# Layer 1's key gather ahead of its first weights; layer 0's parameters and states on ScalarE's queue

## What is computed

```python
for l in range(2):                      # layers
    h = rms_norm(x, norm_g[l])
    a_val, a_glu, a_gate, b_val, b_gate, q, k, v, c_gate = split(h @ w_in[l])   # 384,384,384,256,256,384,384,384,384
    u  = a_val * sigmoid(a_glu)         # conv over 31 positions; the samples use state_conv[l]
    ya = silu(layer_norm(dwconv(concat(conv_buf, u)))) * silu(a_gate)
    yb = pool_linear(trailing_means(concat(pool_buf, b_val)) - b_val) * silu(b_gate)   # samples: state_pool[l]
    q, k = rope(rms_norm(q)), rope(rms_norm(k))
    o  = dilated_attention(q, concat(cache_k, k), concat(cache_v, v))  # distances 0..128, 4*(0..128), 16*(0..128)
    x  = x + concat(ya, yb, o * silu(c_gate)) @ w_out[l]
    # outputs also: conv and pool tails, and both caches of every sample moved on by one position
```

## Time and profile before

| | us |
|---|---|
| median of 3 runs | 431.8 (431.1 to 432.26) |
| the profiled execution | 428.37 |
| its span | 426.5 |
| TensorE busy | 353.0 (83%) |
| VectorE busy | 231.9 (54%) |
| ScalarE busy | 103.4 (24%) |
| mean granted clock of TensorE | 0.943 of 2.4 GHz |
| moved by DMA | 158.06 MB, mean 371 GB/s |

### The profile page before, as it was taken

How to read it: one execution, slowest core, us unless ns; L and a number is a source line. 1 busy time by engine, 2 the same in 40 slices (tenths; PEclk the granted TensorE clock), 3 DMA queues, 4 the chain that set the end, 5 groups by cost and what they waited for, 6 DMA issues and landing times.

```text
span 426.5 us, 4489 instructions
## 1 busy us (share of the span) xinstructions
PE 353.0 (83%) x1552; PEld 273.1 (64%) x1552; DVE 231.9 (54%) x522; ACT 103.4 (24%) x243; POOL 38.1 (9%) x70
## 2 busy tenths in 40 slices
PE   1480099999859896999997999999658988999993
PEld 1360088888647675556886888888446754558872
DVE  1232008997997677542104259989987686341110
ACT  4200010153314342141102101443124332320113
POOL 0698000000000000000000000000009000000000
PEclk9997589999986999999998999999969998999998
DMA  8999999999999999999999999999989999999995
GB/s 295 399 420 418 358 406 343 372 392 415 353 378 416 418 413 373 345 337 362 423 412 379 416 411 412 365 415 382 314 306 380 390 377 339 336 329 325 329 335 231
DMA packets 47301, 158.06 MB, mean 371 GB/s; under 512 B 3861, under 2 KB 16351, under 8 KB 46703
## 3 DMA queue, kind: packets, MB, share of 16 engines
q0 software_dynamic: 22592, 100.62, 63.8%
q1 hardware_dynamic: 16040, 34.40, 22.2%
q10 hardware_dynamic: 8646, 22.76, 13.9%
HBM read 154.90 MB, written 104.42 MB: 608 GB/s over the span
## 4 chain that ended last, share of the span: by engine, by line
PE 57%; DVE 16%; DMA 14%; SPq 6%; ACT 2%; issue 2%; ACTq 0%; DVEq 0%
PE pj L544 28%; PE pj L683 13%; DMA st_pool<-in_state_pool 7%; DMA kv<-in_cache_v_win 7%; PE psc L615 7%; DVE kv L1046 4%; DVE ssc L1049 4%; DVE yc L1106 3%; SPq L394 3%; PE ptr L470 2%; PE ps L492 2%; SPq L371 1%; SPq L386 1%; DVE qk L983 1%; PE ps L666 1%
## 5 line engine op out<-in xcount | busy, mean ns | idle before, releaser
L544 PE MATMUL pj<-hT,w 128*128 128x264 f32 x800 | 195.3, 403 | 2.8 <-DVE hT L968 2.8
L544 PEld LDWEIGHTS pj<-hT,w 128*128 128x128 f32 x800 | 157.5, 200 | 34.5 <-issue 7.0
L1106 DVE SCALAR_TENSOR_TENSOR yc<-u_ext,par,yc 128x256 f32<-128x256 f32 x180 | 76.2, 481 | 2.8 <-DVE u_smp L996 0.6
L683 PE MATMUL pj<-mix,w 128*128 128x264 f32 x256 | 59.2, 386 | 0.0
L683 PEld LDWEIGHTS pj<-mix,w 128*128 128x128 f32 x256 | 48.5, 190 | 8.2
L462 POOL DMA_DIRECT2D out<-in_cache_k_win x32 | 18.5, 586 | 292.1 <-issue 277.7
L1176 DVE TENSOR_TENSOR xT<-xT,pj 128x264 f32<-128x264 f32 x16 | 6.9, 430 | 53.6 <-PE pj L683 53.6
L994 DVE SCALAR_TENSOR_TENSOR u_ext<-ex,pj 128x256 f32<-128x256 f32 x6 | 2.5, 422 | 48.6 <-ACT ex L791 48.6
L615 PE MATMUL psc<-kv,spm 128*48 128x384 f32 x80 | 27.3, 492 | 0.4 <-DMA kv<-in_cache_v_win 0.4
L791 ACT ACTIVATE ex<-pj 128x264 f32<-128x264 f32 x22 | 8.6, 391 | 76.2 <-PE pj L544 68.0
L897 ACT ACTIVATE hT<-xT 128x264 f32<-128x264 f32 x16 | 6.8, 423 | 66.1 <-DVE xT L1176 66.1
(11 more groups left out here) (169 smaller groups left out, 333.9 us busy)
## 6 DMA issues: line engine op xcount, KB each, us to landing
out<-in_cache_k_win POOLq DMA_DIRECT2D x32, 1512.0 KB, 90.5
out<-in_cache_v_win POOLq DMA_DIRECT2D x32, 1512.0 KB, 95.8
w<-in_w_out ACTq DMA_DIRECT2D x2, 4096.0 KB, 27.1
w<-in_w_in ACTq DMA_DIRECT2D x1, 4608.0 KB, 29.8
kv<-in_cache_k_win SPq DMA_DIRECT2D x32, 144.0 KB, 24.6
w<-in_w_in ACTq DMA_DIRECT2D x3, 1536.0 KB, 27.8
kv<-in_cache_v_win SPq DMA_DIRECT2D x32, 144.0 KB, 18.1
w<-in_w_in SPq DMA_DIRECT2D x1, 4608.0 KB, 29.9
```

What stands on the lines that cost most here:

```text
L544: last = nc.tensor.matmul(pj[n % RING][:, 0:T], wbuf[buf][:, k, col:col + P], hT[:, k, :], start=(k == 0), stop=(k == KD - 1))
L683: last = nc.tensor.matmul(pj[n % RING][:, 0:T], w1[:, k, m * P:(m + 1) * P], mix[:, k, :], start=(k == 0), stop=(k == KD - 1))
L1106: last = V.scalar_tensor_tensor(out=yc[:, t, 0:SEQ], in0=x_w, scalar=par[:, ROW_CW + w * CT + t:ROW_CW + w * CT + t + 1], in1=yc[:, t, 0:S ...
```

## The change

- The parameters of layer 0 are issued from ScalarE's queue, ahead of its first computation; its states from the same queue behind the three squares, then the q weights, which now wait for `a_val_in`.
- `st0` and `st1` move from behind projections 1 and 2 to behind 5 and 6, in both layers.
- POOL's bulk copies wait for `a_gate_in` in place of `a_val_in`.
- In layer 1, SP issues the key gather ahead of the `a_` weights; it waits only for the seventh `sc_full` of layer 0. In layer 0 it stays behind the pool weights.

```diff
 _behind = {
-    1: ["st0"], 2: ["st1"], 8: ["sconv"],
+    5: ["st0"], 6: ["st1"], 8: ["sconv"],
...
             weights(0, w0, 0, "w_in", COL["a_val"], 2 * C_CONV, "a_val_in")
-            params(0)
             sp.dma_start(cst[:, early:], const[:, early:]).then_inc(const_in, 16)
 
             for l in range(DEPTH):
                 if l > 0:
+                    sp.wait_ge(S["sc_full"], nth(l - 1, "sc_full", NH + 1))
+                    gather("k", l, "k_in")
                     sp.wait_ge(S["pj_full"], nth(l - 1, "pj_full", NPROJ))
                     weights(l, w0, 0, "w_in", COL["a_val"], 3 * C_CONV, "a_in")
                 else:
                     weights(l, w0, 2 * C_CONV, "w_in", COL["a_gate"], C_CONV, "a_gate_in")
-                if l == 0:
-                    states(l)
...
-                sp.wait_ge(x_copied, XROUNDS)
-                if l > 0:
-                    sp.wait_ge(S["sc_full"], nth(l - 1, "sc_full", NH + 1))
-                gather("k", l, "k_in")
+                if l == 0:
+                    sp.wait_ge(x_copied, XROUNDS)
+                    gather("k", l, "k_in")
...
-            pool.wait_ge(S["a_val_in"], 16)
+            pool.wait_ge(S["a_gate_in"], 16)
...
             nc.scalar.preload_act_table_set(LOG_SET)
 
+            for r0, name, pat in ((ROW_CW, "conv_w", "o w (t c) -> (o w t) c"), (ROW_CB, "conv_b", "o (t c) -> (o t) c"),
+                                  (ROW_LG, "ln_g", "o (t c) -> (o t) c"), (ROW_LB, "ln_b", "o (t c) -> (o t) c"),
+                                  (ROW_PS, "pool_scale", "o (t c) -> (o t) c"), (ROW_NG, "norm_g", "o (t c) -> (o t) c")):
+                src = ins[name][bass.ds(0, 1)].rearrange(pat, c=P)
+                act.dma_start(prow[r0:r0 + src.shape[0], :], src).then_inc(S["par_in"], 16)
+            for r0, name in ((ROW_QN, "q_norm_g"), (ROW_KN, "k_norm_g")):
+                for h in range(2):
+                    act.dma_start(prow[r0:r0 + 1, h * HD:(h + 1) * HD], ins[name][bass.ds(0, 1)]).then_inc(S["par_in"], 16)
+
             act.wait_ge(x_in, 32)
             act.wait_ge(early_in, 16)
...
+            act.dma_start(st_conv[:, :, :], ins["state_conv"][bass.ds(0, 1)].rearrange("o (r s) w c -> (o s w) r c", r=2)
+                          ).then_inc(S["st_in"], 16)
+            act.dma_start(st_pool[:, :], ins["state_pool"][bass.ds(0, 1)].rearrange("o s w c -> (o s w) c")).then_inc(S["st_in"], 16)
+            act.wait_ge(S["a_val_in"], 16)
             weights(0, w1, 0, "w_in", COL["q"], 3 * C_ATT, "q_in")
```

More of the change, by code:

```diff
@@ L379, in params @@
             def params(l):
-                if l > 0:
-                    sp.wait_ge(S["tr_full"], nth(l - 1, "tr_full", TR["par"] + 1))
+                sp.wait_ge(S["tr_full"], nth(l - 1, "tr_full", TR["par"] + 1))
                 for r0, name, pat in ((ROW_CW, "conv_w", "o w (t c) -> (o w t) c"), (ROW_CB, "conv_b", "o (t c) -> (o t) c"),
@@ L391, in states @@
             def states(l):
-                if l > 0:
-                    sp.wait_ge(S["tr_full"], nth(l - 1, "tr_full", TR["st1"] + 1))
+                sp.wait_ge(S["tr_full"], nth(l - 1, "tr_full", TR["st1"] + 1))
                 sp.dma_start(st_conv[:, :, :], one("state_conv", l).rearrange("o (r s) w c -> (o s w) r c", r=2)
```

## The result

The changed kernel takes 447.9 us in the median (444.29 to 455.79, 4 runs) against 431.45 of the kernel before beside it: a ratio of 1.0385, interval 1.0329 to 1.0442. That is slower, as forecast, but by 16.5 us where 7.3 was the sum, and outside the range (431 to 444.5). The profiled execution took 447.06, its span 445.3; from profile to profile that is 18.7 us more than before, where the medians lie 16.5 apart. Every ratio here is worked out from fast runs alone (that of 455.79 us is not among them), and beside the first four experiments only two of seven runs of the kernel before were fast.

What follows compares the result with a forecast made beforehand. TensorE's projections bound the kernel nearly everywhere, with full DMA queues deciding its waits. Layer 0 -27.5, hole ahead of layer 1 +34.6 and clock +0.2 sum to +7.3 us on 431.8: 439 us, range 431 to 444.5.

Steps and rivals of the forecast that it cites:

- its wait moves as it is: Value gather of layer 0: TensorE's wait shifts unchanged with the earlier layer 0, sample values done at 166.7, before 194.2.
- just hidden: Bulk copies start at about 29, end 5.3 us later at about 425, before the last rows of y at 428.
- I take 0.5 off it: Start of layer 0: 0.5 us off the 4.9 us gain, for small packets sharing engines; first projection at about 18.1.
- 4.4 us booked for the parameters' move: Start of layer 0: parameters on ScalarE's queue bring the first projection earlier, gain 4.9 us less 0.5.
- The states: Layer 0: states land within a few us, no hole before projection 2; projection 8 ends at 53.1, 27.5 us earlier.
- the second rival: Layer 0: states land late as before, at 52, costing 10.7 us of the gain; 450 us, chance 0.04.
- I book nothing: Layer 0's key gather lands by 71, VectorE asks at 77.5; six us of cover, so no cost.
- Gather and weights, 72.0 us: Ahead of layer 1: gather issued at 166.7, weights behind it landed at 238.7; TensorE stands 34.6 us.
- 189.2 + 0.2: Layer 1: 189.2 us from its start to the last issue, as before, plus 0.2 us for the clock behind the hole.
- the third rival: End of kernel: bulk copies end last because their start moves by 14.2 us; 441 us, chance 0.09.
- The first rival: Layer 1: weights land in time, layer 0's gain stays; 428 to 430 us, chance 0.11; no change, another 0.11.

Runs made afterwards that it cites:

- the first four experiments: Changed kernel with weights first in layer 1 (1.0201); kernel before with keys first (1.0802); changed kernel with copies early (1.0315); changed kernel with weights first, copies early (1.0141).

## Why the prediction was wrong

The sign and the place were right: the gather ahead of the weights makes a hole ahead of layer 1, ended by `w<-in_w_in`, larger than what layer 0 gains. The order alone, added to the kernel before, costs 8%; taken from the changed kernel, it moves the end of compute by 43.7 us. Without copies it costs nothing, as even turns between small rows and the copies' large ones are what makes the gather slow. The size was wrong in three terms of compute and in the term of the copies. Two steps failed: for the time, "its wait moves as it is", the largest of the three; as reasoning, the copies that stay "just hidden".

- *First projection, "I take 0.5 off it"*: 19.39, not 18.1. The small DMAs took 1.6 us from the prompt and the identity matrix, shown by putting them back. **1.3 us.** Of the 4.4 us booked for the parameters' move, 0.5 were its own.
- *The states*: right, and the second rival falls. They landed within 8.3 us, and projection 8 ended at 54.7. Layer 0 was 26.0 us ahead there, against 27.5.
- *Layer 0's keys, "I book nothing"*: right in effect, with little room. The last piece landed at 48.4 + 28.8 = 77.2, where 71 was forecast, and VectorE asked at 79.0: 1.8 us of cover, not six. With the copies early this cover was gone, and VectorE waited.
- *The value gather, "its wait moves as it is"*: **the largest of the terms, 6.6 us.** It landed 33.6 us behind its last issue, against 29.4, and TensorE's 16 matmuls behind it took 7.47 us at a mean granted clock of 0.71, against 5.33 us at 1.00 before. L614 is at 174.7, not at 166.7. How far this is the change's is open: in four other kernels with the late start of the copies (weights first with one semaphore and with 11, the parameters on SP, the changed kernel with 11) that landing took 31.1 to 31.4 us, and the output projection started at 172.2 to 173.8, against 177.4 here. Some 2 us of the landing are common to them; the rest was seen in this execution only.
- *Gather and weights, 72.0 us*: 75.2 here, 73.2 and 74.6 with the parameters on SP and with 11 semaphores. **3.2 us.** The share was right (39 packets per us beside v's weights, where 39.7 was forecast); q1 moved 2008 packets in 179 to 217, about the gather's 2048, and at 39 per us the weights' 1040 were out by about 244, but they landed at 249.9, where 2 us were booked. The last rows straggled: q1 still moved 0.15, 0.09 and 0.03 MB in 244 to 246, 246 to 248 and 248 to 250.
- 1.3 + 6.6 + 3.2 = 11.1 of the 11.3 us by which layer 1 started later than 238.7. From its start on, 189.6 us to the last issue, against 189.2 + 0.2. So 7.3 + 11.3 + 0.2 = 18.8 us, the difference of the spans; that the medians differ by 2.3 less is because the median before lies 3.1 us above its profiled execution, and the median after only 0.8 above its own.
- ***"Bulk copies", 5.3 us later, "just hidden": the step that failed as reasoning.*** They ended at about 442, not at 425, and in the kernel before at about 423, not at 420: 19 us later. The start itself came at 32.5, not at 29. I took the engines for full while two queues had work; they were busy, but moved less: 304 GB/s in 15 to 20 (403 before), where 1008 of 1029 packets are under 2 KB and the start of the copies matters little (303 with the early one), and 262 and 269 in 30 to 35 and 35 to 40, beside the gather's 12 KB rows. 12.99 MB went in the first 40 us, 15.23 before. And I left out that POOL's second batch waits for the last of the first 46 DMAs: in 320 to 334 the changed kernel moved 160 GB/s. With 11 semaphores and nothing else changed its copies end at 433. I had read the low rate of a lone copy as lack of company on a queue; it is the copy's own, whatever the queue.

So the third rival, "the copies end last, 441", was nearly as true as the forecast. In the changed kernel the two ends lie within 3 us: last issue at 439.5, copies to 442, and the last rows of y behind both, in 443 to 445. So compute's end sets the time, by little. But with the hole taken out it stays at 440.59, slower than before by 2%, and the late start of the copies in the kernel before (with the 11 semaphores, which alone cost nothing) gives that same 2%. For that the change needs no hole. The first rival's price, 428 to 430 if the weights landed in time, is refuted with it: that needs the early start of the copies and the semaphores too (427.62), and then it is no more than before (0.9988).

Open: why the changed kernel takes 1.0385 of before and the one with 11 semaphores 1.0264. They weren't run beside each other, and their intervals overlap (1.0329 to 1.0442, 1.0166 to 1.0362); the stand of POOL may be part of it, and a part of the value gather's lateness was one execution's.

Point by point of what was to show: first projection near 18 (19.4), no hole at projection 2 (yes), L618, here L614, near 167 (174.7), gather right behind it (yes, 174.71), a hole of over 30 us ended by the weights (39.6), first matmul near 239 (249.95), layer 0's keys landed before 77 (77.2, a near miss that cost nothing).

## What to carry to other kernels

The new caches are 100.6 MB in all, two layers of keys and of values at 25.2 MB each, not 50. Alone at 330 GB/s they would take 305 us, which looks like ample room beside 426. It isn't, as the loads share the engines: 158.06 MB in all at the mean of 371 GB/s are 426 us, the whole span of the kernel before. So where a long background copy keeps the DMA engines busy nearly all the time, sum all bytes over the mean rate before you price any wait: if that comes within a few per cent of compute, time taken out of compute is not taken out of the kernel. A late start of the copy then costs even while the engines look busy (8.8 us here for 18.7 of delay), as busy engines can still move less. In a queue whose turns are counted in packets, put few large rows that are needed soon ahead of many small ones that have cover.

## What the runs showed of the hardware

- A copy from DRAM to DRAM moves 318 to 338 GB/s alone, on POOL's queue, on SP's, or on both at once (318 in 410 to 420 with the weights first, 338 in 380 to 400 of the kernel before).
- The gather alone fills the engines' time at 234 GB/s, with rows of 1536 B only at 235 to 253; beside the copy the queues of the earlier trace rows moved 7.17 MB in 20 us, 359 GB/s.
- POOL went on behind its 46th bulk DMA only after waits of 267 to 297 us in seven kernels, when all shared one semaphore, and less than 1 us after that DMA had landed in the three where the landing was read (333.8, 338.4 and 341.1, against 334.59, 339.18 and 341.94); with six on each, it stood 20 to 41 us at a time.
- The first 46 DMAs on one queue ended unevenly: with the weights first and the copies early, q0 moved only 48 packets in the last 10 us of them.
- 480 KB of states issued at 11.6 and 12.0 on ScalarE's queue, ahead of its weights, landed within 8.3 us, with the copies early too (8.8 us). Behind the weights on SP's queue the pooling state, issued at 22.5, took 29.7 us.
